# One-hots and gated parts of the expert gates in runs of two tokens instead of four

## The reference, cut to what matters

```python
e_idx = jnp.take_along_axis(cand_i, pos, axis=-1).reshape(T, PEER_HEADS * PEER_TOPK)
gate = jax.nn.softmax(top_s, axis=-1).reshape(T, PEER_HEADS * PEER_TOPK)
...
ub = jnp.take(peer_u, ib, axis=0).astype(jnp.float32)
a = jnp.einsum('tkd,td->tk', ub, xb.astype(jnp.float32))
a = jax.nn.gelu(a, approximate=False) * gb
vb = jnp.take(peer_v, ib, axis=0).astype(jnp.float32)
return jnp.einsum('tk,tkd->td', a, vb).astype(xb.dtype)
```

## Time and profile before

| | us |
|---|---|
| median of three runs | 3923.16 |
| lowest and highest | 3921.88, 3923.99 |
| the profiled execution | 3925.07 |
| its span | 3923.0 |
| mean granted clock of TensorE | 0.982 |
| PE busy | 3738.8 (95%) |
| DVE busy | 2042.7 (52%) |
| ACT busy | 1404.3 (36%) |

### The profile page before, as it was taken

How to read it: one execution, slowest core, us unless ns; L and a number is a source line. 1 busy time by engine, 2 the same in 40 slices (tenths; PEclk the granted TensorE clock), 3 DMA queues, 4 the chain that set the end, 5 groups by cost and what they waited for, 6 DMA issues and landing times.

```text
span 3923.0 us, 62520 instructions
## 1 busy us (share of the span) xinstructions
PE 3738.8 (95%) x20274; PEld 3428.8 (87%) x20274; DVE 2042.7 (52%) x3704; ACT 1404.3 (36%) x2015; POOL 1045.1 (27%) x457
## 2 busy tenths in 40 slices
PE   4999898999999999999989998989999999999998
PEld 3999898989977888888879997989999778888887
DVE  6497535887746422222246855369875563222223
ACT  2324323333333333333333343333333333333333
POOL 1333223430022222222213321335200222222221
PEclk7999998999999999999999999999999999999999
DMA  5477322334455544444435761323344455444442
GB/s 208 150 249 233 95 83 97 103 117 161 160 171 164 163 152 148 147 145 147 139 117 185 252 205 60 118 86 104 140 158 172 156 168 161 147 147 146 145 148 99
DMA packets 238796, 582.76 MB, mean 149 GB/s; under 512 B 16368, under 2 KB 119152, under 8 KB 234608
## 3 DMA queue, kind: packets, MB, share of 16 engines
q1 hardware_dynamic: 128016, 465.88, 36.1%
q10 hardware_dynamic: 110688, 115.75, 8.7%
HBM read 527.56 MB, written 54.00 MB: 148 GB/s over the span
## 4 chain that ended last, share of the span: by engine, by line
PE 89%; DVE 4%; issue 3%; ACT 2%; POOL 2%; DMA 1%; ACTq 0%; DVEq 0%; SPq 0%; POOLq 0%
PE bank L668 28%; PE bank L449 17%; PE bank L451 17%; PE bank L450 17%; PE bank L645 7%; POOL split_lo L360 1%; PE bank L563 1%; ACT split_hi L355 1%; PE bank L542 1%; PE bank L467 0%; PE bank L596 0%; PE bank L438 0%; DVE h_lo L1162 0%; DVE waste L376 0%; ACT prob L839 0%
## 5 line engine op out<-in xcount | busy, mean ns | idle before, releaser
L360 POOL TENSOR_TENSOR split_lo<-raw,split_hi 128x1024 fp32r<-128x1024 f32 x404 | 993.0, 2458 | 2751.2 <-ACT split_hi L355 2751.1
L449 PE MATMUL bank<-h_hi,split_hi 128*128 128x384 f32 x3712 | 1267.1, 341 | 86.3 <-DVE h_lo L1162 63.8
L355 ACT ACTIVATE split_hi<-raw 128x1024 fp32r<-128x1024 f32 x768 | 813.8, 1060 | 1437.8 <-PE bank L451 1103.8
L451 PE MATMUL bank<-h_hi,split_lo 128*128 128x384 f32 x3712 | 1251.4, 337 | 0.0
L450 PE MATMUL bank<-h_lo,split_hi 128*128 128x384 f32 x3712 | 1250.9, 337 | 0.0
L360 DVE TENSOR_TENSOR split_lo<-raw,split_hi 128x1024 fp32r<-128x1024 f32 x364 | 451.1, 1239 | 1207.0 <-ACT split_hi L355 1206.6
L449 PEld LDWEIGHTS bank<-h_hi,split_hi 128*128 128x128 f32 x3712 | 704.1, 190 | 123.2 <-DVE h_lo L1162 79.1
L450 PEld LDWEIGHTS bank<-h_lo,split_hi 128*128 128x128 f32 x3712 | 704.1, 190 | 6.5
L451 PEld LDWEIGHTS bank<-h_hi,split_lo 128*128 128x128 f32 x3712 | 703.4, 189 | 0.0
L668 PE MATMUL bank<-split_hi,a_hi 128*128 128x512 f32 x1536 | 491.7, 401 | 9.1 <-DVE a_lo L1522 9.1
L668 PE MATMUL bank<-split_hi,a_lo 128*128 128x512 f32 x1536 | 485.3, 397 | 0.0
(11 more groups left out here) (163 smaller groups left out, 2594.7 us busy)
## 6 DMA issues: line engine op xcount, KB each, us to landing
raw<-panels SPq DMA_DIRECT2D x768, 512.0 KB, 3.3
mod_raw<-mod_panels SPq DMA_DIRECT2D x96, 512.0 KB, 4.4
gates_spilled<-kept ACTq DMA_DIRECT2D x24, 2048.0 KB, 6.4
spilled<-gates_spilled ACTq DMA_DIRECT2D x64, 768.0 KB, 5.9
raw<-mod_panels SPq DMA_DIRECT2D x16, 512.0 KB, 3.4
bias<-bias_in ACTq DMA_DIRECT2D x16, 256.0 KB, 2.6
dft<-dft_in ACTq DMA_DIRECT2D x2, 1218.0 KB, 8.6
silu_c<-c_in ACTq DMA_DIRECT2D x2, 1024.0 KB, 4.5
```

The costliest lines, as they stand in the source:

```text
L355: nc.scalar.activation(col(split_hi, s % 2, D), col(raw, s, D), ACT.Copy).then_inc(hi_ready[s], 1)
L360: eng.tensor_tensor(col(split_lo, s % 2, D), col(raw, s, D), col(split_hi, s % 2, D).bitcast(F32), ALU.subtract).then_inc(lo_ready[s], 1)
L449: mm(out, w_hi, col(rhs_hi, kk, n), start=(kk == 0), stop=False)
L451: last = mm(out, w_lo, col(rhs_hi, kk, n), start=False, stop=(kk == KT - 1))
```

## The change

A run is now two tokens (`RUN` = 2), and a tile has two runs (`RUNS`). Within each one-hot and each gated part the order becomes run, key, token of the run, so neighbouring keys of one token lie two bf16 apart, 4 bytes. The buffers stay as large as they were; `index` halves. `route_t` is stored tile by tile, the four first keys and then the four second keys, so that the comparison stays one operation over four groups of two tokens. The product becomes two operations, one for each run; the semaphore is raised by the second. The matmuls are as many as before, with the new steps.

```diff
--- before.py
+++ after.py
@@ -82,6 +82,8 @@
 PROJ = FIRST["peer"]
 
 TILE_T = 4
+RUN = 2
+RUNS = TILE_T // RUN
 NT = T // TILE_T
 CHUNK_T = 32
 CHUNKS = T // CHUNK_T
@@ -188,7 +190,7 @@
     hot_at = o
     hot, o = place("hot", o, HOTS * HOT, BF16)
     hot_end = o
-    index, o = place("index", o, TILE_T * P, BF16)
+    index, o = place("index", o, RUN * P, BF16)
     route_t, o = place("route_t", o, 2 * T, BF16)
     gate_t, o = place("gate_t", o, PARTS * T, BF16)
     spilled, peer_end = place("spilled", o, 2 * BLOCK * T)
@@ -379,11 +381,11 @@
 
     def hot_pair(r):
 
-        return hot[:, r * HOT:r * HOT + 2 * TILE_T * P].rearrange("p (k j t) -> p k j t", k=2, t=TILE_T)
+        return hot[:, r * HOT:r * HOT + 2 * TILE_T * P].rearrange("p (k g j t) -> p k g j t", k=2, g=RUNS, t=RUN)
 
     def hot_parts(r):
 
-        return hot[:, r * HOT + 2 * TILE_T * P:(r + 1) * HOT].rearrange("p (c j t) -> p c j t", c=PARTS, t=TILE_T)
+        return hot[:, r * HOT + 2 * TILE_T * P:(r + 1) * HOT].rearrange("p (c g j t) -> p c g j t", c=PARTS, g=RUNS, t=RUN)
 
     block_cm = nc.Block()
     block = block_cm.__enter__()
@@ -639,10 +641,10 @@
                 pe.wait_ge(gate_copied, l * NT + n + 1)
                 keys2, parts = hot_pair(r), hot_parts(r)
                 for t in range(TILE_T):
-                    w = keys2[:, 1, :, t]
+                    w = keys2[:, 1, t // RUN, :, t % RUN]
                     o = col(bank[2 + r], t, P)
                     for c in range(PARTS):
-                        last = mm(o, w, parts[:, c, :, t], start=(c == 0), stop=(c == PARTS - 1))
+                        last = mm(o, w, parts[:, c, t // RUN, :, t % RUN], start=(c == 0), stop=(c == PARTS - 1))
                 last.then_inc(gate_mm, 1)
 
             carry(pe)
@@ -930,8 +932,9 @@
 
             def store_route(t):
                 act.wait_ge(route_tr, l * TT + t + 2)
-                copy(route_t[:, 0:2 * T].rearrange("p (j t) -> p j t", j=2)[:, :, bass.ds(t * P, P)],
-                     bank[4][:, 0:2 * P].rearrange("p (j t) -> p j t", j=2))
+                copy(route_t[:, 0:2 * T].rearrange("p (n k t) -> p k n t", k=2, t=TILE_T)
+                     [:, :, bass.ds(t * (P // TILE_T), P // TILE_T), :],
+                     bank[4][:, 0:2 * P].rearrange("p (k n t) -> p k n t", k=2, t=TILE_T))
                 copy(gate_t[:, bass.ds(t * P, P)], col(bank[4], 2, P))
                 copy(gate_f[:, bass.ds(t * P, P)], col(bank[4], 2, P)).then_inc(route_stored, 1)
 
@@ -1375,8 +1378,8 @@
             norm(2 * l + 2)
             modulate(l, 1)
 
-            order.step(V.tensor_copy(index[:, :].rearrange("p (j t) -> p j t", t=TILE_T),
-                                     iota[:, :].unsqueeze(2).broadcast_to([P, P, TILE_T])), hold=True)
+            order.step(V.tensor_copy(index[:, :].rearrange("p (j t) -> p j t", t=RUN),
+                                     iota[:, :].unsqueeze(2).broadcast_to([P, P, RUN])), hold=True)
 
 
             with dve.Fori(0, COUNT["pq"]) as i:
@@ -1483,21 +1486,25 @@
             def keys_hot(n, r):
 
                 dve.wait_ge(gate_mm, l * NT + n + 1)
-                shape = [P, 2, P, TILE_T]
-                V.tensor_tensor(hot_pair(r),
-                                index[:, :].rearrange("p (j t) -> p j t", t=TILE_T).unsqueeze(1).broadcast_to(shape),
-                                route_t[:, 0:2 * T].rearrange("p (k t) -> p k t", k=2)
-                                [:, :, bass.ds(n * TILE_T, TILE_T)].unsqueeze(2).broadcast_to(shape),
+                shape = [P, 2 * RUNS, P, RUN]
+                V.tensor_tensor(hot[:, r * HOT:r * HOT + 2 * TILE_T * P]
+                                .rearrange("p (g j t) -> p g j t", g=2 * RUNS, t=RUN),
+                                index[:, :].rearrange("p (j t) -> p j t", t=RUN).unsqueeze(1).broadcast_to(shape),
+                                route_t[:, bass.ds(n * (2 * TILE_T), 2 * TILE_T)]
+                                .rearrange("p (g t) -> p g t", t=RUN).unsqueeze(2).broadcast_to(shape),
                                 ALU.is_equal).then_inc(eq_ready, 1)
 
             def gated_hot(n, r):
 
                 dve.wait_ge(eq_ready, l * NT + n + 1)
-                shape = [P, PARTS, P, TILE_T]
-                V.tensor_tensor(hot_parts(r), hot_pair(r)[:, 0, :, :].unsqueeze(1).broadcast_to(shape),
-                                gate_t[:, 0:PARTS * T].rearrange("p (c t) -> p c t", c=PARTS)
-                                [:, :, bass.ds(n * TILE_T, TILE_T)].unsqueeze(2).broadcast_to(shape),
-                                ALU.mult).then_inc(hot_ready, 1)
+                shape = [P, PARTS, P, RUN]
+                for g in range(RUNS):
+                    last = V.tensor_tensor(hot_parts(r)[:, :, g, :, :],
+                                           hot_pair(r)[:, 0, g, :, :].unsqueeze(1).broadcast_to(shape),
+                                           gate_t[:, 0:PARTS * T].rearrange("p (c t) -> p c t", c=PARTS)
+                                           [:, :, bass.ds(n * TILE_T + g * RUN, RUN)].unsqueeze(2).broadcast_to(shape),
+                                           ALU.mult)
+                last.then_inc(hot_ready, 1)
 
             def hot_group(i, last=False):
                 for s in range(SLOTS):
```

## The result

| | before | after |
|---|---|---|
| median, us | 3923.57 | 3823.18 |
| lowest and highest | 3921.88, 3927.82 | 3821.36, 3825.28 |
| runs | 4 | 4 |
| the profiled execution | 3925.07 | 3825.28 |
| its span | 3923.0 | 3823.2 |

The ratio is 0.9743 with a 95% interval of 0.9726 to 0.976: 100 us less, where 107 had been forecast (3816, range 3800 to 3868).

A forecast was written before the change was run, and what follows sets the result against it. TensorE (PE) was taken to bound the gate stage. Steady intervals, first group and last group save 49.9 + 0.6 + 2.9 = 53.4 us a layer, 106.8 in both, giving 3816 us; range 3800 to 3868.

The forecast's parts named there:

- PE sets the stage: Gate matmul stage, 24 groups a layer: PE alone sets the interval, 48c + 4.21 us, c being the time per matmul.
- The matmul's price: Gate matmuls on PE: time follows bytes walked at 8.75 per ns, so 0.118 us falls to 0.0585 at 4-byte steps.
- Rival B: Gate matmuls: a floor per load and matmul pair between 0.0585 and 0.110 us; 3848 us at the middle; chance 0.14.
- Rival C: Gate matmuls: the weight load, 117 ns record, holds them at 0.118 us, the step costs nothing; 3923 us; chance 0.08.
- Rival D: DVE's keys and products lose the pace of two elements a step with runs of two; 4051 us; chance 0.10.
- The new wait: PE ahead of every fourth tile waits for gated parts queued on DVE behind the next keys: 0.58 us an interval.
- The first group of a layer: Start of each layer's gate stage: paced by DVE, 9.56 us against 10.19, a gain of 0.63 less 0.07.
- the steady interval: From one gate group to the next, 22 a layer: 9.87 us falls to 7.60, saving 49.9 us a layer.
- The last group: End of each layer's gate stage: no next keys ahead of its gated parts, PE at full pace, 2.87 us gained.

The follow-up runs named there:

- the weights' steps: Changed kernel with PE reading the weights of a tile's four tokens at steps of 2, 8, 16, 32 bytes, moving columns at 4: 3829.6 us.
- The swap: Changed kernel with DVE doing the gated parts ahead of the next tile's keys at the last tile of each group of four: 3804.7 us, ratio 0.9692.
- the first experiment: Changed kernel with PE reading the moving columns of a tile's four tokens at steps of 2, 8, 16, 32 bytes, weights at 4: 4104.6 us.

## Why the prediction was right, point by point

**PE sets the stage; what the change is worth is its time per matmul.** Shown by the result and by the two products in the kernel before, where DVE's added work moved nothing.

**The matmul's price.** 0.0585 was forecast, 0.057 measured. The step behind it, memory walked at 8.75 bytes per ns, was right for every row it was read from and wrong as a law: the price is per 16-byte line, 1.8 ns, so it stops at 16 bytes, and one column a cycle ends it from below. Steps of 4 and 8 bytes fill each line evenly, so bytes and lines gave the same number here: that the wrong law priced this step rightly is luck, and at 32 bytes it would have been out by a factor of two. The floor of one column a cycle, put at 0.053 as the lower bound, measured 0.057 and lies at the very step of the change, so next to nothing is left below it.

**Rival B**, a floor per pair up to 0.110, did not show: pairs ran at 0.057. The Trainium skill's 81 ns, "TensorE: Matmul & The Clock Gate", Back-to-back issue gap, is higher than the 57 measured here for 128 columns with a load each. **Rival C**, the weight load, fell with the weights' steps. **Rival D** did not occur; its price was right where it was made to occur.

**The new wait.** The chain from the end of tile 4 to the start of tile 7 was forecast at 1.99 us; the rows after give (with a tile's end taken at 12 x 0.057, as for before: 932.68 + 0.68 = 933.36) 0.33 to the keys, 0.61 to the first product, 0.47 to the second, 0.55 for it and 0.06 to PE: 2.02. The interval was forecast at 7.60 and came out at 7.62 in these rows. The swap shows that the order makes it.

**Where 7 of the 107 us went.** The sum missed in two terms. The first group of a layer was forecast to be paced by DVE at the full clock, 9.56 us to the next group against 10.19 before. The 10.19 was read from the chain, where a piece starts when the one ahead of it ends; by matmul starts the first interval before was 861.91 - 851.88 = 10.0, so 0.17 of the forecast 0.63 was never there. After, it took 10.07 (853.55 to 863.62) and 11.0 in layer 1 (2732.29 to 2743.29): a gain of 0.6 each became a loss of 0.1 and 1.0. The clock, which the sum had put at its full level, is the other part. The rows of the first tiles after show it: at a granted clock of 0.50, 12 matmuls take 1.46 us, (1.46 - 0.31) / 11 = 0.105 each, close to one column a cycle at 1.2 GHz (0.107), so the four tiles forecast at 5.35 took 5.82 (853.55 to 859.37); in layer 1 the panel behind also ran partly at that level (0.79 from 2738 to 2743 us). Before, the same start cost less, because matmuls held by their reads do not feel the clock: in the first group, at 0.50, 10 matmuls took 1.36 us, (1.36 - 0.30) / 9 = 0.118 each, as at full clock. The first tile after, then of before a part of the first group, its stretch (columns as above) and the start of the second group:

```profile
853.55 1.46 PE L647 MATMUL bank<-hot 128*128 128x128 bf16 x12 [3.37 <-DVE hot L1502]
...
853.46 1.36 PE L645 MATMUL bank<-hot 128*128 128x128 bf16 x10
853.40:856.20 2.80, 2.80 (x25) 2.55 (x24) 2.80 (x5) 1.20 (x2) 0.00 (x0) 0.50 0.00 0
...
861.91 1.34 PE L645 MATMUL bank<-hot 128*128 128x128 bf16 x10
```

The kernel before read at 4 bytes has both cases in one profile, the first group of layer 0 and that of layer 1:

```profile
848.80:853.90 5.10, 4.44 (x48) 3.75 (x49) 5.10 (x7) 1.79 (x3) 0.00 (x0) 0.67 0.01 3
2727.80:2733.40 5.60, 5.57 (x48) 4.78 (x49) 5.60 (x8) 1.79 (x3) 0.00 (x0) 0.50 0.02 4
```

At 0.67 its first interval is 9.36 us (848.83 to 858.19), at 0.50 it is 10.11 (2727.78 to 2737.89).

The first term is 2.3 us of the 7. The second is the steady interval: from 863.62 to the last group at 1032.15 are 22 intervals of 7.66 in the mean, not 7.60, 2.7 us in both layers. Most of them are 7.62 to 7.64, the last three 7.5; every fourth, where PE's loop over panels turns, is longer (878.90 to 886.70, 7.80). PE's rows of such an interval, the panel's start in another one, and the branch of the loop on PE's weight-load queue:

```profile
878.90 1.26 PE L647 MATMUL bank<-hot 128*128 128x128 bf16 x19
...
881.59 0.86 PE L647 MATMUL bank<-hot 128*128 128x128 bf16 x12 [0.45 <-DVE hot L1502]
882.45 0.41 PE L451 MATMUL bank<-h_hi,split_hi 128*128 128x384 f32 x1
...
886.70 1.49 PE L647 MATMUL bank<-hot 128*128 128x128 bf16 x23
...
936.05 0.42 PE L451 MATMUL bank<-h_hi,split_hi 128*128 128x384 f32 x1
...
L651 PEldq COMPARE_BRANCH  x12: 76/212/225, 881.7 to 2913.8; - x12
```

The extra time lies on PE between the fourth tile and the panel: 882.45 - 881.59 = 0.86 us from the tile's start to the panel's, against 936.05 - 935.38 = 0.67 where the loop does not turn, and the branch at 881.7 falls into it. Before, the branch took as long (208 ns at the median) and no interval stood out (9.85 to 9.89 from the second on); that the slower matmuls covered it is my reading, and no run tells it apart. The last group gave 2.84 us as forecast (2.87). The remaining 2 us lie outside the stage, where the kernels do the same: the first Fourier matmuls, far ahead of the change, already start at 497.4 us in the profiled execution after and at 495.3 in that of before. So they are not the change's.

## What to carry to other kernels

Count the 16-byte lines that a matmul's moving columns touch: a line cost 1.8 ns here, a column 0.45 at the full clock, so four columns a line are enough, two cost double, and the weights' step hardly matters. A layout that serves TensorE must leave DVE two adjacent elements in its innermost run: runs of two gave both engines their pace here, runs of one cost DVE half of its own. When the bound engine gets faster, look for the operation that waits in a neighbour's queue ahead of the one it needs: moving one operation past another gave 18 us more here than the layout alone.

## What the runs showed of the hardware that was not expected

- The reads of a matmul's moving columns cost 1.8 ns a 16-byte line: 0.117 us for 64 lines, 0.233 for 128, whether columns lie 16 or 32 bytes apart.
- TensorE's granted clock fell to 0.50 while PE was busy without a gap, behind matmuls held up by their reads (5.50 us of 5.50 busy at 0.50), and the panel that followed ran its first half at that level. With all gate matmuls at 0.118 us the clock of the stage had been 0.99. In the stage with runs of one, where PE waited up to 2.2 us ahead of a tile, the clock was 0.76 in the mean.
- Matmuls held by their reads did not slow down with the clock: 0.118 us each at 0.50 and at 0.99; in the first experiment's tile at 0.50 those at 16 bytes kept 0.23 us, while those at 2 bytes went from 0.057 to 0.107.
- A weight load's record of 146 ns did not keep matmuls from following each other every 0.06 us.
